# Layer 0 of a two-layer backbone: conv slice pieces ahead of retention, conv taps between the decay products

## The chip, the cores and the metric

One core of one Trainium2 chip. The metric is the device time of one execution in microseconds (us). The kernel before was run three times: 1911.14, 1915.06 and 1921.12 us, median 1915.06. Its profiled execution is a fourth one.

## The reference, cut to what matters

Two layers over 256 latent tokens and 256 context tokens with 1024 features. Each layer normalizes and modulates, projects once to three groups of heads, mixes each group, projects back, and adds; then comes a dense (layer 0) or an expert (layer 1) channel mixer. The three groups:

```
p = h @ w_in[l]                       # 2304 columns; the last 512 are conv value and conv gate
# retention, 4 heads of 64, for the latents and (layer 0 only) for the context:
a = einsum('bcihd,bcjhd->bchij', qc, kc) * dmat     # scores times a decay by distance
inner = einsum('bchij,bcjhe->bcihe', a, vc)
# conformer convolution, 256 channels, 31 taps:
h = a * sigmoid(gt)
h = conv_general_dilated(h, w, 31 taps, padding 15) + bias      # one filter per channel
h = silu(layernorm(h) * ln_w + ln_b)
# windowed attention with 8 query and 2 key/value heads
```

Layer 0 needs all of this for both streams (latents are stream 0, context is stream 1 in token order), layer 1 for the latents only. Everything is float32; a big product is made of three products of high and low parts (high x high, high x low, low x high).

## The kernel before, in words

Each engine has its own program, written out in order by hand, and semaphores between them. No planner orders anything: what stands first in an engine's program is done first.

**Banks.** Eight PSUM banks. VectorE empties banks 0 to 3 (VB), ScalarE banks 4 to 6 (AB), bank 7 (OB) is kept for attention. From the last slice of the input projection on, bank 3 is taken out of VectorE's ring and belongs to the conv slice, so three stay for the rest.

**The conv slice** (`conv_slice`, a Python generator of TensorE's program) makes the 512 conv columns with channels on the partitions. For each channel tile `ct` (128 channels each) it makes first the gate (half 1), then the value (half 0): four groups that all go through bank 3, each of 8 values of `k` with three matmuls each. It yields after every second `k`, so a group is four pieces and a piece is 6 matmuls of 512 columns; 16 pieces in all. The caller says with `next(conv)` where each piece goes. The first half of the rows of the weights is one item (`k` 0 to 3), the second half another; an item can be used when ScalarE has written its high part and VectorE its low part (`split_to`, the subtraction is line 1692). ScalarE empties a gate group with a sigmoid into SC (`conv_gate`), VectorE a value group by multiplying it with SC into the padded buffer CB (`conv_value`). Each group waits until the one before it has been emptied (semaphore `conv_gone`).

**Order of TensorE in layer 0**: projection slices; 2 pieces; `turn_heads`, the transposes of the conv filter and of the retention queries and keys (RT); 2 pieces; `states`, the decayed state of the context; 2 pieces; `retention`; `attention`. In `retention`, for each of the two streams: 1 piece, scores of heads 0 and 1, then for each head (with the scores of heads 2 and 3 ahead of head 1) 1 piece and `apply`, which multiplies the decayed scores AD of a head with its values. `apply` waits for VectorE's decay product of that head. Then `turn_qk` (transposes for attention) and the products with the states.

**Order of VectorE in layer 0**: the copies of the filter (convw) and of RT, the scaling of the decay table, the state copies, then for each stream four decay products `AD = scores * decay`, with `conv_value(0)` behind the first one, and taps behind some. A tap (line 1905) is one instruction over 512 tokens of 128 channels of the first channel tile (`CA = CB[shifted] * w + CA`), 31 in all, each waiting for the one before it. 17 taps stand behind decay products (9 behind head 3 of stream 0, 2 and 6 behind heads 1 and 3 of stream 1), 2 behind `conv_value(1)`, 12 in the first nine steps of attention (`TAPS`). The second channel tile is shared by ScalarE (products, line 1371) and GpSimd (adds, line 1663); it starts in attention and has no part in the change, though its adds run beside the taps. Behind the 14th add GpSimd computes the reciprocal roots for the retention readout (line 1624), for which VectorE's readout waits.

**Attention** is 16 steps `m` of two heads each in layer 0: scores (line 771), maximum on VectorE (line 2009), exponential on ScalarE, transposes (line 779), products with the values (line 790), and between them products with the modulation weights (line 561), whose 1 MB items arrive through four slots.

Of the kernel before, what the change touches and what calls it, by code (L numbers as in the profile page):

```python
# [43 lines left out]
PRODUCTS = 4  # L44
ADA_ITEMS = ((2, 1, 2, 1, 2, 1, 2, 1, 2, 2, 2, 2, 2, 2, 0, 0), (2, 3, 2, 3, 2, 2, 2, 0))
ADA_SLOTS = (0, 1, RAW, RAW + 1)
EARLY_TAPS = ({(0, 3): 9, (1, 1): 2, (1, 3): 6}, {(0, 1): 6, (0, 3): 10})
LAST_EARLY = (2, 3)
TAPS = ((2, 2, 2, 1, 1, 1, 1, 1, 1), (3, 3, 3, 3))
PRODUCT_TAPS = ((3, 3, 3, 3, 3, 3, 3, 3, 3, 3, 1), (6, 6, 6, 6, 6, 1))  # L50
READOUT = (1, 1)
CONV_TURN = (11, 6)
# [62 lines left out]
def build(nc, io, place):  # L115
    ctx = ExitStack()
    with ctx:
# [15 lines left out]
        _, YS_t = phase(("gap_ys", TT * D_MODEL, F32), ("YS", 2 * D_MODEL, F32R))  # L133
# [64 lines left out]
        for group, row_kb in ((0, 92), (1, 27), (2, 27)):  # L198
            _, row_t[group] = phase((f"gap_row{group}", row_kb * KB, F32), (f"row{group}", SLICE, F32))
        _, RT_t = phase(("gap_RT", 76 * KB, F32), ("RT", 8 * KB, F32))  # L200
        _, more0_t, _, more1_t = phase(("gap_more0", 104 * KB, F32), ("more0", 8 * KB, F32), ("gap_more1", 8 * KB, F32), ("more1", 8 * KB, F32))
        _, PT_t = phase(("gap_PT", 64 * KB, F32), ("PT", 8 * KB, F32))
        _, CA0_t = phase(("gap_CA0", 92 * KB, F32), ("CA0", 2 * KB, F32))
        _, distance_t = phase(("gap_distance", 80 * KB, F32), ("distance", 4 * KB, F32))
# [7 lines left out]
        _, heads_t, _, hTf_t, _, xn_t = phase(  # L212
            ("gap_heads", 96 * KB, F32), ("heads", 8 * KB, F32), ("gap_hTf", 24 * KB, F32), ("hTf", 16 * KB, F32),
            ("gap_xn", 12 * KB, F32), ("xn", 16 * KB, F32))

        _, SG_t, YG_t, _, HFr_t, HF_t = phase(
            ("gap_sg", 88 * KB, F32), ("SG", 4 * KB, F32), ("YG", 4 * KB, F32), ("gap_hfr", 32 * KB, F32),
            ("HFr", 44 * KB, F32R), ("HF", 4 * KB, F32))
# [6 lines left out]
        _, xnx_t = phase(("gap_xnx", 24 * KB, F32), ("xnx", 8 * KB, F32))  # L225
        _, hx0_t, _, hx1_t = phase(("gap_hx0", 88 * KB, F32), ("hx0", 4 * KB, F32), ("gap_hx1", 80 * KB, F32), ("hx1", 4 * KB, F32))
        _, hxc_t = phase(("gap_hxc", 72 * KB, F32), ("hxc", 8 * KB, F32))
# [254 lines left out]
        def _(pe):  # L482
# [220 lines left out]
                mm.then_inc(v_full, 1)  # L703

            def retention(layer, conv):
                pieces = 1 if layer == 0 else 2

                def scores(s, h):
                    b = open_v(("decayed", layer, s, h))
                    lo = 64 * (h % 2)  # L710
                    for jt in range(TT):
                        mm = nc.tensor.matmul(b[:, jt * SEQ:(jt + 1) * SEQ],
                                              RT[lo:lo + 64, 2 + h // 2, s * TT + jt, :],
                                              RT[lo:lo + 64, h // 2, s * TT:s * TT + TT, :].rearrange("p t n -> p (t n)"),
                                              start=True, stop=True)
                    mm.then_inc(v_full, 1)

                def apply(s, h, outs):
                    pe.wait_ge(v_done, job[("decayed", layer, s, h)] + 1)
                    for it in range(TT):  # L720
                        for jt in range(TT):
                            mm = nc.tensor.matmul(outs[it][:, h * 64:(h + 1) * 64],
                                                  AD[:, h, jt * SEQ + it * P:jt * SEQ + (it + 1) * P],
                                                  proj[:, s * TT + jt, C_RV + h * 64:C_RV + (h + 1) * 64],
                                                  start=(jt == 0), stop=(jt == TT - 1))
                        if h == RET_HEADS - 1:
                            mm.then_inc(a_full, 1)

                pe.wait_ge(v_done, n_v[0])
                for s in ((0, 1) if layer == 0 else (0,)):  # L730
                    for _ in range(pieces):
                        next(conv)
                    scores(s, 0)
                    scores(s, 1)
                    outs = [open_a(("inner", layer, s)), open_a()]
                    for h in range(RET_HEADS):
                        if h == 1:
                            scores(s, 2)
                            scores(s, 3)
                        for _ in range(pieces):  # L740
                            next(conv)
                        apply(s, h, outs)
                assert next(conv, None) is None
                turn_qk(layer)

                for t in range(TT):
                    b = open_v()
                    for pair in range(2):
                        mm = nc.tensor.matmul(b[:, pair * 256:(pair + 1) * 256], RT[:, pair, t, :], ST[:, pair, :],
                                              start=True, stop=True)  # L750
                    mm.then_inc(v_full, 1)
# [400 lines left out]
            for layer in range(DEPTH):  # L1152
                streams = (0, 1) if layer == 0 else (0,)
                if layer == 0:
                    after(cond_ready)
                    for i in range(2 * EARLY):
                        ada_product()
                        if i:
                            turn_normalized((0, 1), i - 1, i)
                    after(bias_in, 16)  # L1160
                    after(rows_out)
                    fold_rows(0)
                    turn_vectors()
                    turn_normalized((0, 1), KT - 1, KT)
                project_in(layer)
                conv = conv_slice(layer)
                next(conv), next(conv)
                turn_heads(layer)
                next(conv), next(conv)
                states()  # L1170
                next(conv), next(conv)
                retention(layer, conv)
                attention(layer)
                project_out(layer)
                if layer == 0:
                    dense_ffn()
# [68 lines left out]
        def _(act):  # L1245
# [229 lines left out]
            for layer in range(DEPTH):  # L1475
# [54 lines left out]
                def conv_gate(ct):  # L1530
                    act.wait_ge(conv_full, CONV_OUTS * layer + 2 * ct + 1)
                    nc.scalar.activation(SC[:, ct, 0:ncol], VB[3][:, 0:ncol], ACT.Sigmoid).then_inc(conv_gone, 1)
# [3 lines left out]
                gates = proj[:, 0:nt, C_RG:C_CONV]  # L1536
                nc.scalar.activation(gates, gates, ACT.Silu).then_inc(rg_ready, 1)
                conv_gate(0)
                if layer:
                    conv_gate(1)  # L1540
                for s in ((0, 1) if layer == 0 else (0,)):
                    for t in range(TT):
                        copy_out(RO[:, s * TT + t, :], take()[:, 0:256])
                    if layer == 0 and s == 0:
                        conv_gate(1)
                for t in tiles:
                    copy_out(AQT[:, :, t, :], take()[:, :].rearrange("p (r n) -> p r n", r=4))
                attention(layer, att_base + NT)
# [129 lines left out]
        def _(dve):  # L1678
# [16 lines left out]
            def take():  # L1695

                n = n_v[0]
                n_v[0] += 1
                dve.wait_ge(v_full, n + 1)
                return v_bank[n]  # L1700
# [8 lines left out]
            def copy_out(out, src):  # L1709
                nc.vector.tensor_copy(out, src).then_inc(v_done, 1)  # L1710
# [197 lines left out]
            def retention(layer, base):  # L1908
# [11 lines left out]
                def conv_value(ct):  # L1920
                    ns = 2 if layer == 0 else 1
                    dve.wait_ge(conv_full, CONV_OUTS * layer + 2 * ct + 2)
                    tt(CB[:, ct, 0:ns, CONV_WIDTH // 2:CONV_WIDTH // 2 + SEQ], VB[3][:, 0:ns * SEQ].rearrange("p (s n) -> p s n", s=ns),
                       SC[:, ct, 0:ns * SEQ].rearrange("p (s n) -> p s n", s=ns), ALU.mult).then_inc(conv_gone, 1)

                copy_out(convw[:, :, :], take()[:, 0:64].rearrange("p (c k) -> p c k", c=2)[:, :, 0:CONV_WIDTH])
                for t in tiles:
                    copy_out(RT[:, :, t, :], take()[:, :].rearrange("p (b n) -> p b n", b=4))

                after(dexp_out, 2)  # L1930
                nc.vector.tensor_scalar(dec[:, :], dec[:, :], HEAD_DIM ** -0.5, None, ALU.mult)
# [3 lines left out]
                step(nc.vector.memset(ST, 0.0))  # L1935
                nc.vector.tensor_copy(ST[0:64, :, 0:P], b[0:64, :].rearrange("p (c n) -> p c n", c=2)[:, :, 0:P])
                copy_out(ST[64:128, :, P:2 * P], b[64:128, :].rearrange("p (c n) -> p c n", c=2)[:, :, P:2 * P])
                after(pad_ready)
                for s in ((0, 1) if layer == 0 else (0,)):
                    if s:  # L1940
                        dve.wait_ge(a_full, full[("inner", layer, 0)] + 2)
                    for h in range(RET_HEADS):
                        tt(AD[:, h, :], take()[:, :], decay[:, h, :], ALU.mult).then_inc(v_done, 1)
                        if s == 0 and h == 0:
                            conv_value(0)
                        if (s, h) in EARLY_TAPS[layer]:
                            early_taps(EARLY_TAPS[layer][s, h])
                conv_value(1)
                early_taps(LAST_EARLY[layer])
                dve.wait_ge(att_done, base)  # L1950
                after(mask_in, 16)
# [416 lines left out]
```

## Time and profile before

| | us |
|---|---|
| median of 3 runs | 1915.06 |
| profiled execution | 1919.19 |
| its span, first to last instruction | 1917.4 |
| PE (TensorE matmul) busy | 1822.6 |
| DVE (VectorE) busy | 1339.3 |
| ACT (ScalarE) busy | 1050.9 |
| POOL (GpSimd) busy | 119.9 |

The names in the rows: PE is the matmul side of TensorE and PEld its weight load, DVE is VectorE, ACT is ScalarE, POOL is GpSimd. The retention of layer 0 lies at 138 to 167 us of the span, its attention from there to about 260 us. Busy shares over the whole span tell nothing of these stretches, which the windows show one by one.

### The profile page before, as it was taken

What the parts mean: (1) busy time and instruction counts of PE and PEld (TensorE: products, weight loads), DVE (VectorE), ACT (ScalarE), POOL (GpSimd) and SP (SyncE); (2) the same over time, 40 slices, a digit from 0 to 9 for tenths busy, and PEclk for the clock granted to TensorE, in tenths of its full rate; (3) what the DMA queues carried; (4) which work ended last, traced back from release to release, by engine and by line L of the source; (5) the groups of instructions that cost most, each with busy time, mean ns of one, the idle gap of its engine ahead of it and who ended that gap; (6) DMA issues with size and microseconds to landing.
All of it is one profiled execution on the core that took longest, in us unless ns stands there. A gap on an engine that the chain in (4) does not pass through costs nothing.

```text
span 1917.4 us, 23772 instructions
## 1 busy us (share of the span) xinstructions
PE 1822.6 (95%) x8964; PEld 1480.7 (77%) x8964; DVE 1339.3 (70%) x1280; ACT 1050.9 (55%) x1009; POOL 119.9 (6%) x126
## 2 busy tenths in 40 slices
PE   4999899999999999987999999999999999999996
PEld 2986578888888888576888788888888888888885
DVE  2579645333323367756888888889888898898886
ACT  3334644322222153545777776777776776777774
POOL 1123600000000012400000000000000000000000
PEclk8999989999999999997999999999999999999999
DMA  8325823532342234735999999999999999999994
GB/s 291 126 88 207 303 75 78 140 96 86 95 109 83 74 97 132 258 138 175 370 332 354 358 340 345 368 346 354 369 328 362 351 361 359 338 354 352 353 367 154
DMA packets 245911, 472.85 MB, mean 247 GB/s; under 512 B 10546, under 2 KB 60564, under 8 KB 245804
## 3 DMA queue, kind: packets, MB, share of 16 engines
q1 hardware_dynamic: 241712, 468.14, 68.9%
q10 hardware_dynamic: 4092, 3.20, 0.6%
q8 instruction: 77, 1.26, 0.3%
q14 instruction: 30, 0.25, 0.0%
HBM read 470.26 MB, written 1.05 MB: 246 GB/s over the span
## 4 chain that ended last, share of the span: by engine, by line
PE 48%; DMA 21%; DVE 16%; ACT 8%; issue 5%; POOL 2%; SPq 0%; DVEq 0%; ACTq 0%; POOLq 0%
PE bank L543 13%; PE bank L545 13%; PE bank L544 13%; DMA raw<-in_moe_w_gate_dram 10%; DVE parts L1707 9%; ACT parts L1409 6%; DMA raw<-in_moe_w_down_dram 5%; DMA raw<-in_moe_w_up_dram 4%; DMA raw<-in_ada_w_dram 2%; PE bank L561 1%; PE bank L1047 1%; POOL gb L1663 1%; DVE parts L1692 1%; PE bank L790 1%; DVE ACC L2180 1%
## 5 line engine op out<-in xcount | busy, mean ns | idle before, releaser
L1707 DVE TENSOR_TENSOR parts<-raw,parts 128x2048 fp32r<-128x2048 f32 x336 | 764.9, 2289 | 115.0 <-ACT parts L1409 113.9
L1409 ACT ACTIVATE parts<-raw 128x2048 fp32r<-128x2048 f32 x336 | 642.7, 1919 | 260.4 <-DMA raw<-in_moe_w_up_dram 94.9
L543 PE MATMUL bank<-parts,XEr 128*128 128x512 f32 x896 | 357.2, 399 | 8.7 <-DVE parts L1707 6.3
L545 PE MATMUL bank<-parts,XEr 128*128 128x512 f32 x896 | 350.1, 391 | 0.0
L544 PE MATMUL bank<-parts,XEr 128*128 128x512 f32 x896 | 349.4, 390 | 0.0
L1270 ACT ACTIVATE parts<-raw 128x2048 fp32r<-128x2048 f32 (+1 forms) x62 | 113.2, 1831 | 270.2 <-PE bank L545 250.0
L1692 DVE TENSOR_TENSOR parts<-raw,parts 128x2048 fp32r<-128x2048 f32 (+1 forms) x62 | 135.8, 2194 | 138.2 <-ACT parts L1270 137.9
L543 PEld LDWEIGHTS bank<-parts,XEr 128*128 128x128 f32 x896 | 168.7, 188 | 49.9 <-DVE parts L1707 10.3
L545 PEld LDWEIGHTS bank<-parts,XEr 128*128 128x128 f32 x896 | 168.5, 188 | 36.6
L544 PEld LDWEIGHTS bank<-parts,XEr 128*128 128x128 f32 x896 | 168.9, 188 | 32.6
L543 PE MATMUL bank<-parts,HTr 128*128 128x512 f32 x448 | 175.6, 392 | 1.3 <-DVE HTr L1707 0.8
L544 PE MATMUL bank<-parts,HTr 128*128 128x512 f32 x448 | 174.5, 390 | 0.0
L545 PE MATMUL bank<-parts,HTr 128*128 128x512 f32 x448 | 174.4, 389 | 0.0
L543 PE MATMUL bank<-hTr,parts 128*128 128x512 f32 (+1 forms) x432 | 164.1, 380 | 7.4 <-ACT hTf L1342 3.7
L544 PE MATMUL bank<-hTr,parts 128*128 128x512 f32 (+1 forms) x432 | 161.8, 375 | 0.0
L545 PE MATMUL bank<-hTr,parts 128*128 128x512 f32 (+1 forms) x432 | 161.8, 375 | 0.0
L543 PE MATMUL bank<-parts,hTr 128*128 128x512 f32 (+1 forms) x320 | 122.0, 381 | 7.3 <-DVE hTr L1707 3.3
L544 PE MATMUL bank<-parts,hTr 128*128 128x512 f32 (+1 forms) x320 | 120.3, 376 | 0.0
L545 PE MATMUL bank<-parts,hTr 128*128 128x512 f32 (+1 forms) x320 | 120.2, 376 | 0.0
L1707 DVE TENSOR_TENSOR HF<-bank,SG 128x512 f32<-128x512 f32 x22 | 15.2, 691 | 138.2 <-PE bank L545 138.2
L543 PEld LDWEIGHTS bank<-parts,HTr 128*128 128x128 f32 x448 | 84.1, 188 | 21.9 <-issue 2.0
L543 PEld LDWEIGHTS bank<-hTr,parts 128*128 128x128 f32 x432 | 81.9, 190 | 24.2 <-issue 7.2
(245 smaller groups left out, 2289.7 us busy)
## 6 DMA issues: line engine op xcount, KB each, us to landing
raw<-in_moe_w_gate_dram SPq DMA_DIRECT2D x112, 1024.0 KB, 7.2
raw<-in_moe_w_up_dram SPq DMA_DIRECT2D x112, 1024.0 KB, 7.2
raw<-in_moe_w_down_dram SPq DMA_DIRECT2D x112, 1024.0 KB, 6.7
raw<-in_ada_w_dram SPq DMA_DIRECT2D x28, 1024.0 KB, 8.0
more<-in_ada_w_dram SPq DMA_DIRECT2D x20, 1024.0 KB, 7.7
raw<-in_w_in_dram SPq DMA_DIRECT2D x12, 1024.0 KB, 5.1
raw<-in_ffn_w_gate_dram SPq DMA_DIRECT2D x22, 512.0 KB, 4.0
raw<-in_ffn_w_up_dram SPq DMA_DIRECT2D x22, 512.0 KB, 5.4
```

What stands on the lines that cost most here:

```text
L543: nc.tensor.matmul(out, st[0], mv[0], start=start, stop=False)
L544: nc.tensor.matmul(out, st[0], mv[1], start=False, stop=False)
L545: return nc.tensor.matmul(out, st[1], mv[0], start=False, stop=stop)
L561: mm = nc.tensor.matmul(b[32 * j:32 * j + 32, :], cond[:, half * KT // 2 + j, c0:c0 + 32], w[:, j, :], start=opening, stop=closing)
L790: mm = nc.tensor.matmul(OB[:, head * 64:(head + 1) * 64], PT[:, n % 4, kb * P:(kb + 1) * P], proj[:, kb, C_V + 64 * g:C_V + 64 * g + 64], ...
L1047: mm = nc.tensor.matmul(M[k // 4][:, (k % 4) * P:(k % 4 + 1) * P], xn[:, t, k * P:(k + 1) * P], PA[:, t, bass.ds(i * 2 + j, 1), :].rearran ...
L1270: nc.scalar.activation(parts[:, s, 0, 0:k * width], raw[:, r, 0:k * width], ACT.Copy).then_inc(hi_ready, 1)
L1409: nc.scalar.activation(parts[:, n % PARTS, 0, :], raw[:, r, :], ACT.Copy).then_inc(hi_ready, 1)
L1663: nc.gpsimd.tensor_tensor(acc, acc, CP[:, k % PRODUCTS, 0:ns, :], ALU.add).then_inc(pool_tap, 1)
L1692: nc.vector.tensor_tensor(parts[:, s, 1, 0:k * width], raw[:, r, 0:k * width], parts_f[:, s, 0, 0:k * width], ALU.subtract).then_inc(lo_re ...
L1707: return nc.vector.tensor_tensor(out, a, b, op)
L2180: nc.vector.scalar_tensor_tensor(acc, M[h][:, :], share[:, ee % 2, t:t + 1], acc, ALU.mult, ALU.add)\
```

## The change

In layer 0, 12 conv pieces stand ahead of retention (4 ahead of `turn_heads`, 4 ahead of `states`, 4 behind it), and retention has 4, all in its first stream: one ahead of the scores and one ahead of `apply` of heads 0, 1 and 2. Both sigmoids of the conv gate stand together in ScalarE's program. VectorE makes `conv_value(0)` right behind the copies of RT, and `conv_value(1)` behind head 3's decay product of stream 0. Taps stand behind every decay product: 3, 4, 4, 5 in stream 0 and 4, 4, 4, 1 in stream 1, then 2 more; none is left in attention. Layer 1 has the same order of instructions as before.

```diff
-EARLY_TAPS = ({(0, 3): 9, (1, 1): 2, (1, 3): 6}, {(0, 1): 6, (0, 3): 10})
+EARLY_TAPS = ({(0, 0): 3, (0, 1): 4, (0, 2): 4, (0, 3): 5, (1, 0): 4, (1, 1): 4, (1, 2): 4, (1, 3): 1}, {(0, 1): 6, (0, 3): 10})
-TAPS = ((2, 2, 2, 1, 1, 1, 1, 1, 1), (3, 3, 3, 3))
+TAPS = ((), (3, 3, 3, 3))
@@ retention, TensorE
-                pieces = 1 if layer == 0 else 2
+                between = iter((1, 1, 1, 1, 0, 0, 0, 0, 0, 0) if layer == 0 else (2, 2, 2, 2, 2))
...
-                    for _ in range(pieces):
+                    for _ in range(next(between)):
                         next(conv)
                     scores(s, 0)
                     scores(s, 1)
...
-                        for _ in range(pieces):
+                        for _ in range(next(between)):
                             next(conv)
                         apply(s, h, outs)
@@ layer loop, TensorE
-                next(conv), next(conv)
+                pieces = range(2 if layer else 4)
+                for _ in pieces:
+                    next(conv)
                 turn_heads(layer)
-                next(conv), next(conv)
+                for _ in pieces:
+                    next(conv)
                 states()
-                next(conv), next(conv)
+                for _ in pieces:
+                    next(conv)
@@ ScalarE
                 conv_gate(0)
-                if layer:
-                    conv_gate(1)
+                conv_gate(1)
...
-                    if layer == 0 and s == 0:
-                        conv_gate(1)
@@ retention, VectorE
                 for t in tiles:
                     copy_out(RT[:, :, t, :], take()[:, :].rearrange("p (b n) -> p b n", b=4))
+                if layer == 0:
+                    after(pad_ready)
+                    conv_value(0)
...
-                after(pad_ready)
+                if layer:
+                    after(pad_ready)
...
-                        if s == 0 and h == 0:
+                        if s == 0 and h == 0 and layer:
                             conv_value(0)
+                        if s == 0 and h == 3 and layer == 0:
+                            conv_value(1)
                         if (s, h) in EARLY_TAPS[layer]:
                             early_taps(EARLY_TAPS[layer][s, h])
-                conv_value(1)
+                if layer:
+                    conv_value(1)
```

## Rows read from the trace of the kernel before

**Rows 1.** The head of the page.

```profile
span 1917.4 us, 23772 instructions
```

**Rows 2.** Windows: PE, PEld, DVE, ACT, POOL busy us, PEclk, DMA share, GB/s.

```profile
138.00:151.00 13.00, 13.00 (x79) 10.62 (x78) 9.83 (x14) 0.77 (x2) 0.00 (x0) 1.00 0.01 1
151.00:162.00 11.00, 11.00 (x69) 9.13 (x69) 8.56 (x13) 0.60 (x1) 0.00 (x0) 1.00 0.00 0
...
180.00:195.00 15.00, 12.25 (x92) 6.77 (x91) 14.69 (x30) 11.16 (x29) 13.73 (x9) 1.00 1.04 384
```

**Rows 3.** Timeline: start us, us, engine, line, what; ahead of retention.

```profile
123.17 0.39 PE L543 MATMUL bank<-hTr,parts 128*128 128x512 f32 x1
...
125.66 0.39 PE L545 MATMUL bank<-hTr,parts 128*128 128x512 f32 x1
...
125.80 2.29 DVE L1692 TENSOR_TENSOR parts<-raw,parts 128x2048 fp32r<-128x2048 f32 x1 [4.19 <-ACT parts L1270]
...
128.28 1.26 PE L675 MATMUL bank<-const,proj 128*128 128x128 f32 x8 [0.96 <-DVE convw L1710]
```

**Rows 4.** Timeline of retention, to the first attention scores (L771).

```profile
138.03 1.14 PE L712 MATMUL bank<-RT 64*128 64x256 f32 x8
...
139.26 0.69 DVE L1707 TENSOR_TENSOR AD<-bank,decay 128x512 f32<-128x512 f32 x1 [3.63 <-PE bank L712]
...
144.01 0.55 DVE L1902 TENSOR_SCALAR CA<-CB,convw,vcols 128x512 f32<-128x512 f32 x1
...
144.59 6.26 DVE L1905 SCALAR_TENSOR_TENSOR CA<-CB,convw,CA 128x512 f32<-128x512 f32 x8
...
151.12 0.60 ACT L1532 ACTIVATE SC<-bank 128x512 f32<-128x512 f32 x1 [1.06 <-PE bank L545]
...
152.25 1.29 DVE L1707 TENSOR_TENSOR AD<-bank,decay 128x512 f32<-128x512 f32 x2 [1.40 <-PE bank L712]
...
161.42 1.09 PEld L722 LDWEIGHTS bank<-proj,AD 128*128 128x128 f32 x8
...
161.85 0.69 DVE L1707 TENSOR_TENSOR CB<-bank,SC 128x512 f32<-128x512 f32 x1 [0.27 <-PE bank L545]
...
166.50 0.76 PE L771 MATMUL bank<-AKT,heads 64*128 64x256 f32 x4
```

**Rows 5.** Groups by line from 168 to 212 us: count, busy us, mean ns, idle before.

```profile
L1905 DVE SCALAR_TENSOR_TENSOR CA<-CB,convw,CA 128x512 f32<-128x512 f32 x12 | 12.0, 999 | 0.1
```

**Rows 6.** The chain of waits in attention: start us, us, what.

```profile
175.21 1.28 POOL gb L1663
...
180.12 2.09 POOL gb L1663
...
187.65 1.68 POOL gb L1663
```

**Rows 7.** Timeline of attention, columns as in rows 3.

```profile
173.79 23.42 POOL L1663 TENSOR_TENSOR gb<-gb,QK 128x512 f32<-128x512 f32 x14 [54.58 <-ACT QK L1371]
...
197.59 2.91 POOL L1624 TENSOR_TENSOR lnr<-lnt,nhalf 128x16 f32<-128x16 f32 x1
...
200.53 2.28 DVE L1707 TENSOR_TENSOR RO<-RO,lnr 128x1024 f32<-128x1024 f32 x1 [4.47 <-POOL lnr L1624]
...
204.59 0.58 ACT L1356 ACTIVATE hTr<-bank 128x512 fp32r<-128x512 f32 x1
...
205.81 0.68 DVE L1707 TENSOR_TENSOR hTr<-bank,hTr 128x512 fp32r<-128x512 f32 x1
...
206.54 1.12 PE L779 MATMUL bank<-const,SC 128*128 128x128 f32 x4 [2.09 <-DVE hTr L1707]
```

**Rows 8.** Windows of 2 us, columns as in rows 2.

```profile
202.00:204.00 2.00, 0.67 (x2) 0.29 (x2) 1.90 (x7) 0.52 (x2) 1.93 (x1) 1.00 1.05 400
...
206.00:208.00 2.00, 1.46 (x8) 1.46 (x8) 2.00 (x2) 2.00 (x7) 1.86 (x2) 0.50 0.15 44
...
212.00:214.00 2.00, 2.00 (x12) 0.75 (x9) 1.79 (x2) 1.99 (x6) 1.86 (x2) 0.96 0.84 246
```

## The prediction

> **What bounds the kernel now.** I read the page first, for the span of the one profiled execution [rows 1], and then the windows, to find which engine is full where the change is made. From 138 to 162 us, layer 0's retention, TensorE is busy in every one of 24 us at the full clock, while VectorE is busy in 9.83 of the first 13 and 8.56 of the last 11 [rows 2]. So this stretch ends when TensorE has gone through its list. In the attention that follows it is the other way round: from 180 to 195 us VectorE is busy in 14.69 of 15 us and GpSimd in 13.73, TensorE in 12.25. The chain of waits puts that stretch on GpSimd: the adds of the second channel tile follow each other without a gap from 173.79 us, 14 of them in 23.42 us, then its power operation (2.91 us from 197.59), and VectorE waits 4.47 us for that before the readout's multiplication at 200.53 [rows 7]. From 206.54 us TensorE is dense again. All the weights of later layers are asked for when earlier ones are used up, so I take a delay here as passed on to the end in full.
>
> **What the change does to the order.** TensorE issues the same instructions; 13 instead of 7 conv pieces (6 matmuls each) now stand ahead of the first scores, 3 instead of 9 behind them. VectorE runs the same 31 taps, but 28 instead of 17 ahead of the last decay product of retention, 3 instead of 2 behind it, none instead of 12 in attention. Layer 1 keeps its order.
>
> **Term 1, the way to the first decay product.** Twelve matmuls go from 123.17 to 125.66 us, first to last start, so one costs 0.226 us and a piece 1.36 us [rows 3]. Six more pieces: +8.15 us. The third and fourth piece are now issued ahead of the head transposes, and they read the second half of the conv weights, whose low part VectorE finishes at 125.80 + 2.29 = 128.09 us; TensorE would go on at 125.89, so it stands for 2.2 us in a place where it used to do the transposes. In return the transposes no longer wait for the convw copy, which stands behind that same split on VectorE: -0.96 us [rows 3]. The thirteenth piece is the first of the fourth group and needs the conv bank emptied by the sigmoid (0.60 us, [rows 4]); nothing stands between it and the twelfth now. The end of the last matmul (0.39 - 0.23), 0.60 and two handovers make 0.86 us of standing. Other new waits are covered: the fifth piece's sigmoid by the transposes, the ninth's product on VectorE by the state matmuls. VectorE's scaling of the decay table and the state copies come behind that product, about 3 us of work, under four pieces (5.4 us) of TensorE. Sum: 8.15 + 2.2 - 0.96 + 0.86 = +10.25 us; the first decay product moves from 139.26 to about 149.5 us. I give this +-1.
>
> **Term 2, from the first to the last product.** Now VectorE's list is the longer one. A tap costs 6.26 / 8 = 0.78 us, the first one 0.58, a product 1.29 / 2 = 0.645, the gating product 0.61 (161.85 to the next start) [rows 4]. In order: 28 taps (0.58 + 27 x 0.78 = 21.7), 8 decay products (5.2) and one gating product (0.6): 27.5 us. TensorE has 3 pieces, 4 pairs of scores at 1.1 us and 7 applications at about 1.1 us in the same time, 16 us, each ready before VectorE comes to the product that reads it, so it hides behind VectorE and waits. The last product ends at 149.5 + 27.5 = 177.0, and the last application starts at 177.1 instead of 161.42: +15.7 us. In the stretch before, the idle third of VectorE paid for 19 taps; now the idle comes first (while 13 pieces run) and can't be used, as the first tap stands behind the first product in program order.
>
> **Term 3, the tail.** From the last application to the first scores of attention it is 5.08 us (161.42 to 166.50) [rows 4]. The last three taps lie beside it. But TensorE comes to this tail rested: in the second stream it works about 4 us in 14, in stretches of 1 to 2 us between waits of up to 3. The trace has a like case: after waits of 2.2 and 2.1 us with a burst between them (0.67 us busy from 202 to 204) the granted clock stands at 0.50 from 206 to 208, the lower level, 1.2 GHz, and is back by 212 to 214, at 0.96 [rows 8]. If it is low through the tail, some 5.6 us of wall time do half the work: +2.8 us at most. If it happens to be high, 0. I take +2.0, nearer to the like case. The Trainium skill ("TensorE: Matmul & The Clock Gate", Part 1) puts the fall down to an idle engine and the return to sustained work. By it alone, waits broken by bursts might keep the clock up, and the sum would be 2.0 smaller; the trace shows a fall after broken waits.
>
> **Term 4, what attention gives back.** The 12 taps take 12.0 us of VectorE there, 1.00 us each instead of 0.78 [rows 4, 5]. They would be worth all of it if VectorE set the end, but it stands 4.5 us for GpSimd at 200.5, so what counts is how much earlier GpSimd's fourteenth add ends. An undisturbed add has a pitch of 175.21 - 173.79 = 1.42 us; fourteen would take 19.9 instead of 23.42, a surplus of 3.5 [rows 6, 7]. Two of the adds are stretched from 1.28 to 2.09 beside the readout's 1024 wide operations, which stay: 1.6. The rest, 1.9 us, is that of the taps (an add beside one takes 1.68) [rows 6]. After it one more tap pair stands ahead of the low part at 205.81, whose high part ScalarE has at 204.59 + 0.58 = 205.17, and TensorE's next transposes wait for it until 206.54 [rows 7]: 0.6 us. Together -2.5 us. Bounds: nothing, if the modulation weights' transfers set the pace instead (DMA share 1.04 from 180 to 195 [rows 2]); -12.0, if VectorE did. Behind 206.54 TensorE is the bound and the last three taps of attention are free. The Trainium skill ("SBUF — State Buffer", SBUF: two separate sides) says that a VectorE instruction with two SBUF inputs and a GpSimd one that reads SBUF exclude each other for a whole instruction. The trace agrees in kind (1.28 grows to 1.68 and 2.09), but by that rule the nine taps ahead of the fourteenth add would return 9 x 0.78 = 7.0 us instead of 1.9 (an estimate from that page's rule), and the chain holds a surplus of only 3.5.
>
> **Sum.** 15.7 + 2.0 - 2.5 = +15.2 us. The profiled execution took 1919.19 us around a span of 1917.4 [rows 1]; it would become 1934.4. The median of the three runs, 1915.06, is 4.1 lower, and by that the forecast is 1930.3 us. Of this the 15.7 is sure within 1.5, as it is counted out of repeated rows.
>
> **Rivals.**
> Attention gives back everything, not slower than before. VectorE is full from 180 to 195, its little scale instructions there grow too, and if it, not GpSimd, sets the pace, 12.0 us of taps go and with them some 3 us of stretched small operations. Then 15.7 + 0 - 15.0 = +0.7, 1915.8 us. It decides at the readout's multiplication: if VectorE no longer finds itself waiting for the power operation there, this is the case. Against it stands that wait of 4.5 us in the trace of before, which any time saved on VectorE alone would only lengthen. 6 in 100.
> The port is given back in full (the rule above, as a mechanism here): each of nine taps had kept GpSimd for 0.78: 15.7 + 2.0 - 7.0 - 0.6 = +10.1, 1925.2 us. Against it: the surplus in the chain. 7 in 100; a mixture of this and the first rival somewhere near 1921, another 6.
> The clock doesn't fall in the second stream: 15.7 - 2.5 = +13.2, 1928.3 us. 22 in 100.
> Transfers hold the attention: four modulation slots are full at its start as before, but if GpSimd lets go earlier, TensorE meets weights that haven't landed. Then nothing is given back: 15.7 + 2.0 = +17.7, 1932.8 us. 15 in 100. With a clock that falls again in attention up to 1936. 4 in 100.
> The forecast itself, 40 in 100, from 1928 to 1933.
>
> **How the numbers follow.** All cases from the clock rival to the transfers lie at +12 to +19; below them lie 19 in 100, of which the port case is inside. So the range is 1922 to 1936. A measurement of this kernel can't tell less than 0.5%, 9.6 us, from nothing. Slower than 1924.6: the forecast, clock and transfers (81) and most of the port case (5), 86 in 100. Within 0.5%: the first rival, the mixture and the rest of the port case, 14. I take 2 and 1 off these for a mechanism that I don't see, by which it would be faster: 84, 13 and 3.
>
> **What would show it.** In the profile after: TensorE idle for about 2 us near 126 to 128; the first decay product near 149.5; from there to about 179.5 a VectorE without a gap and TensorE with waits for decay products of 2 to 3 us, their sum about 12; granted clock below 1 somewhere from 165 to 182; the first attention scores near 182 to 185 instead of 166.5; fourteen GpSimd adds in about 21.5 us instead of 23.4. I am wrong if the first product comes by 145, if taps between products cost less than 0.78, or if the distance from the first attention scores to the dense part (40 us before) shrinks by more than 5.

## The result and the profile after

The changed kernel is slower: median 1933.12 us (five runs, 1926.80 to 1936.10) against 1913.76 us (five runs, 1911.14 to 1921.12), ratio 1.0085 with a 95% interval of 1.0064 to 1.0106, so +16.3 us (12 to 20) on 1913.76. The two medians by themselves are 19.4 us apart, inside that interval. Forecast was +15.2, 1930.3 us, slower.

The profiled execution of the changed kernel took 1926.80 us, the fastest of its five; its span is only 7.6 us longer than before's. So the spans of two profiles don't give the size. The stages do. First the timeline around retention, which answers to rows 3 and 4 (start us, us, engine, line, what):

```profile
126.20 2.29 DVE L1693 TENSOR_TENSOR parts<-raw,parts 128x2048 fp32r<-128x2048 f32 x1 [4.20 <-ACT parts L1274]
...
128.55 0.50 PE L543 MATMUL bank<-hTr,parts 128*128 128x512 f32 x1 [2.10 <-DVE parts L1693]
...
147.27 0.47 PE L543 MATMUL bank<-hTr,parts 128*128 128x512 f32 x1 [0.78 <-ACT SC L1536]
...
149.99 0.69 DVE L1708 TENSOR_TENSOR AD<-bank,decay 128x512 f32<-128x512 f32 x1 [7.11 <-PE bank L712]
...
153.35 3.10 DVE L1906 SCALAR_TENSOR_TENSOR CA<-CB,convw,CA 128x512 f32<-128x512 f32 x4
...
160.73 1.10 PE L722 MATMUL bank<-proj,AD 128*128 128x64 f32 x8 [2.52 <-DVE AD L1708]
...
165.83 1.94 PE L722 MATMUL bank<-proj,AD 128*128 128x64 f32 x8 [2.00 <-DVE AD L1708]
...
172.98 1.97 PE L722 MATMUL bank<-proj,AD 128*128 128x64 f32 x8 [1.29 <-DVE AD L1708]
...
175.86 0.68 DVE L1708 TENSOR_TENSOR AD<-bank,decay 128x512 f32<-128x512 f32 x1
176.46 2.32 DVE L1906 SCALAR_TENSOR_TENSOR CA<-CB,convw,CA 128x512 f32<-128x512 f32 x3
...
176.60 1.97 PE L722 MATMUL bank<-proj,AD 128*128 128x64 f32 x8 [1.65 <-DVE AD L1708]
...
184.31 0.75 PE L771 MATMUL bank<-AKT,heads 64*128 64x256 f32 x4
```

VectorE stands for 7.11 us ahead of the first decay product, at 149.99 instead of 139.26, and from there runs product, taps, product, taps to 178.8 without a gap. TensorE waits for products, and an application takes 1.94 to 1.97 us in the second stream; in the kernel before it takes 1.00, as in the last one there:

```profile
161.65 1.00 PE L722 MATMUL bank<-proj,AD 128*128 128x64 f32 x8
```

The windows of the changed kernel show why (busy us of PE, PEld, DVE, ACT, POOL, PEclk, DMA share, GB/s):

```profile
155.00:160.00 5.00, 3.22 (x23) 2.70 (x21) 4.86 (x8) 0.00 (x0) 0.00 (x0) 1.00 0.26 74
160.00:165.00 5.00, 3.10 (x16) 2.18 (x16) 4.86 (x9) 0.77 (x2) 0.00 (x0) 0.68 0.91 345
165.00:170.00 5.00, 4.17 (x18) 3.28 (x18) 4.86 (x9) 0.00 (x0) 0.00 (x0) 0.50 0.00 0
170.00:175.00 5.00, 3.65 (x16) 3.27 (x16) 4.86 (x7) 0.00 (x0) 0.00 (x0) 0.50 0.00 0
175.00:180.00 5.00, 3.40 (x16) 3.40 (x17) 3.67 (x6) 1.30 (x3) 0.00 (x0) 0.50 0.00 0
180.00:185.00 5.00, 5.00 (x28) 4.18 (x26) 1.97 (x3) 1.85 (x4) 0.00 (x0) 0.77 0.02 3
```

VectorE is at 4.86 of 5, TensorE at 3.1 to 3.2 of 5. A window of 1 us, below, has the granted clock fall just ahead of 162, behind the wait of 2.52 us and the application after it; from there it is at 0.50, 1.2 GHz, until it rises again at about 182:

```profile
161.00:162.00 1.00, 1.00 (x10) 0.93 (x11) 0.97 (x3) 0.51 (x2) 0.00 (x0) 0.92 1.02 365
```

Now attention, which answers to rows 7:

```profile
191.59 21.52 POOL L1664 TENSOR_TENSOR gb<-gb,QK 128x512 f32<-128x512 f32 x14 [71.98 <-ACT QK L1375]
213.19 0.21 POOL L1624 TENSOR_SCALAR lnt<-lnv 128x16 f32<-128x16 f32 x1
213.48 2.91 POOL L1625 TENSOR_TENSOR lnr<-lnt,nhalf 128x16 f32<-128x16 f32 x1
...
216.42 2.28 DVE L1708 TENSOR_TENSOR RO<-RO,lnr 128x1024 f32<-128x1024 f32 x1 [7.29 <-POOL lnr L1625]
...
221.84 1.31 PE L779 MATMUL bank<-const,SC 128*128 128x128 f32 x4 [1.15 <-DVE hTr L1708]
...
244.66 1.13 PE L771 MATMUL bank<-AKT,heads 64*128 64x512 f32 x4
```

The fourteen adds take 21.52 instead of 23.42 us, and VectorE, freed of its taps, waits longer for GpSimd: 7.29 instead of 4.47 us [rows 7].

To compare kernels I use the start of the scores of step 12 of attention, in a part where TensorE is dense in all of them: 229.64 us before, 244.66 after, +15.0. Of this 0.40 us is there ahead of all changed code: the split of the conv weights' second half (L1692, in the changed kernel L1693) starts at 126.20 instead of 125.80 [rows 3]. Counted from the split, step 12 is 14.6 us later. Behind it the code is unchanged. GpSimd's clearing of the accumulator ahead of the experts stands at 886.72 before and 904.68 after, +18.0: 3 us more came in without a changed instruction. In the timeline of the changed kernel:

```profile
904.68 1.80 POOL L1675 MEMSET ACC<- 128x2048 f32 x1 [10.33 <-DVE top L1708]
```

From there to the end it was 1030.7 us before and 1020.3 after. In the eight experiments, which all have the same code there, this last part took between 1022.4 and 1035.0 us in one profile each. That spread, not the change, is what separates the two spans' difference of 7.6 from the stage's 15.

### The profile page after: what moved, and what is told of

The parts are those of the page before. It is cut to its first block, busy times and chain, and to the rows that moved or that the text cites. A ratio compares the mean times of both kernels' runs of the same rounds, so it can differ in the third digit from the quotient of the medians.

```text
span 1925.0 us, 23773 instructions
## 1 busy us (share of the span) xinstructions
PE 1828.7 (95%) x8964; PEld 1491.7 (77%) x8964; DVE 1333.5 (69%) x1280; ACT 1051.4 (55%) x1009; POOL 117.3 (6%) x126
## 3 DMA queue, kind: packets, MB, share of 16 engines
HBM read 470.26 MB, written 1.05 MB: 245 GB/s over the span
## 4 chain that ended last, share of the span: by engine, by line
PE 82%; DVE 7%; DMA 3%; ACT 3%; issue 2%; POOL 2%; SPq 0%; DVEq 0%; ACTq 0%; POOLq 0%
PE bank L543 24%; PE bank L544 24%; PE bank L545 24%; PE bank L1047 2%; DMA raw<-in_ada_w_dram 2%; PE bank L561 2%; PE bank L1101 1%; DMA raw<-in_moe_w_gate_dram 1%; DVE parts L1693 1%; DVE parts L1708 1%; PE bank L790 1%; POOL gb L1664 1%; DVE CA L1906 1%; ACT parts L1413 1%; PE bank L779 1%
## 5 line engine op out<-in xcount | busy, mean ns | idle before, releaser
L1693 DVE TENSOR_TENSOR parts<-raw,parts 128x2048 fp32r<-128x2048 f32 (+1 forms) x62 | 135.7, 2193 | 138.8 <-ACT parts L1274 138.5
L544 PE MATMUL bank<-parts,HTr 128*128 128x512 f32 x448 | 174.5, 390 | 0.0
L1708 DVE TENSOR_TENSOR HF<-bank,SG 128x512 f32<-128x512 f32 x22 | 15.2, 691 | 138.2 <-PE bank L545 138.2
```

Source lines behind the costliest of these rows:

```text
L544: nc.tensor.matmul(out, st[0], mv[1], start=False, stop=False)
L1693: nc.vector.tensor_tensor(parts[:, s, 1, 0:k * width], raw[:, r, 0:k * width], parts_f[:, s, 0, 0:k * width], ALU.subtract).then_inc(lo_re ...
L1708: return nc.vector.tensor_tensor(out, a, b, op)
```

## The experiments

They ran in two groups of four, each group on one chip with runs of the kernel before between them (16 and 23), against which the ratios are taken; heads_early and after_ro10 ran only once. The table has, from the profiles, the start of the first decay product, the end of the last one, the first attention scores, and the scores of step 12 (its difference to before), the same difference counted from each profile's own split, then the ratio over all runs.

| kernel | first product | last product ends | first scores | step 12 | from the split | whole kernel |
|---|---|---|---|---|---|---|
| before | 139.26 | 156.98 | 166.50 | 229.64 | 0 | 1 |
| after | 149.99 | 176.54 | 184.31 | 244.66 (+15.0) | +14.6 | 1.0085 [1.0064, 1.0106] |
| pieces_only | 149.76 | 170.62 | 180.52 | 243.82 (+14.2) | +14.0 | 1.0066 [1.0044, 1.0088] |
| taps_only | 139.53 | 167.17 | 172.17 | 233.47 (+3.8) | +3.5 | 1.0023 [1.0007, 1.0038] |
| fill_waits | 150.18 | 176.74 | 181.75 | 243.53 (+13.9) | +13.3 | 1.0070 [1.0040, 1.0101] |
| heads_early | 149.64 | 176.21 | 184.00 | 244.45 (+14.8) | +14.5 | one run |
| taps_ahead | 148.94 | 168.49 | 175.86 | 237.62 (+8.0) | +8.6 | 1.0067 [1.0046, 1.0088] |
| after_ro10 | 150.04 | 176.59 | 184.59 | 244.65 (+15.0) | +14.5 | one run |
| before_ro10 | 139.79 | 157.51 | 167.03 | 229.22 (-0.4) | -0.9 | 0.9987 [0.9968, 1.0006] |
| best | 139.05 | 156.77 | 166.29 | 227.39 (-2.3) | -2.0 | 0.9989 [0.9975, 1.0004] |

The split itself starts between 125.16 and 126.41 us, with the same code ahead of it in all ten profiles, so a bare start can be off by more than 1 us. Counted from the split, the first product repeats: 13.45 to 13.48 us in the four kernels with the pieces as before, 23.76 to 23.79 in five of the six with the pieces in front.

**pieces_only**: which half of the change costs?

```diff
-EARLY_TAPS = ({(0, 0): 3, (0, 1): 4, (0, 2): 4, (0, 3): 5, (1, 0): 4, (1, 1): 4, (1, 2): 4, (1, 3): 1}, {(0, 1): 6, (0, 3): 10})
-TAPS = ((), (3, 3, 3, 3))
+EARLY_TAPS = ({(0, 3): 9, (1, 1): 2, (1, 3): 6}, {(0, 1): 6, (0, 3): 10})
+TAPS = ((2, 2, 2, 1, 1, 1, 1, 1, 1), (3, 3, 3, 3))
```

> The changed kernel with the taps back where the kernel before has them (9, 2 and 6 behind products, 2 behind the last value, 12 in attention); only the 12 pieces in front, the two sigmoids together and the places of the two gating products stay. Theory (VectorE's serial list after a late first product): first decay product near 150.0 as in the changed kernel; TensorE done with the first stream by 159; VectorE waits for the fourth conv group until 157.3, then 9 taps to 165, products of stream 1 with 2 taps between, the last one done near 169.5; first attention scores near 174.5 to 176 (before 166.5, changed 184.3); attention from its first scores to those of step 9 in 46 us as before; step 9 at +8 to +9.5, whole kernel +8 to +10 us. Rival (the taps between the products alone make the loss, pieces in front cost only their stalls of 2 us): first attention scores near 169, whole kernel +2 to +3.

First product and the taps up to 164.5 came as expected, but the first scores at 180.5 instead of 174.5 to 176, and the pieces alone cost +14.2 us, nearly the whole loss. The expectation left out the clock. Timeline and windows of this kernel:

```profile
165.34 1.94 PE L722 MATMUL bank<-proj,AD 128*128 128x64 f32 x8 [5.43 <-DVE AD L1708]
...
169.23 5.38 PE L722 MATMUL bank<-proj,AD 128*128 128x64 f32 x24
```
```profile
160.00:165.00 5.00, 0.00 (x0) 0.00 (x0) 4.82 (x7) 0.00 (x0) 0.00 (x0) 0.67 0.86 323
165.00:170.00 5.00, 4.66 (x20) 3.76 (x20) 2.88 (x6) 0.00 (x0) 0.00 (x0) 0.50 0.00 0
170.00:175.00 5.00, 5.00 (x25) 5.00 (x25) 4.82 (x8) 0.73 (x2) 0.00 (x0) 0.50 0.00 0
```

The block of nine taps holds the first product of stream 1 back, TensorE stands idle for 5.43 us, wakes at half its clock, and has four applications, a pair of scores and the transposes of the tail still before it, with no long wait between them to absorb that. That the clock makes the difference is read from these windows; fill_waits tests it on the changed kernel, no run does on this one.

**taps_only**: the other half.

```diff
-EARLY_TAPS = ({(0, 3): 9, (1, 1): 2, (1, 3): 6}, {(0, 1): 6, (0, 3): 10})
-TAPS = ((2, 2, 2, 1, 1, 1, 1, 1, 1), (3, 3, 3, 3))
+EARLY_TAPS = ({(0, 0): 3, (0, 1): 4, (0, 2): 4, (0, 3): 5, (1, 0): 4, (1, 1): 4, (1, 2): 4, (1, 3): 1}, {(0, 1): 6, (0, 3): 10})
+TAPS = ((), (3, 3, 3, 3))
```

> The kernel before with only the taps moved (3, 4, 4, 5, 4, 4, 4, 1 behind the products, then 2), pieces as before. Theory: first product at 139.3 as before; VectorE's list from there is 26.6 us of taps and products plus some 1.5 us of waits for the first value and for scores, last product done near 167.7 instead of 157.0, last application there instead of 161.4; first attention scores near 172.9, up to 2 more if the clock falls; attention to step 9 2.5 us shorter than before; step 9 at +4 to +6, whole kernel +4 to +6 us. Rival (the taps in attention are worth their 12 us, or hide in retention): whole kernel -2 to -6.

As the theory had it: last product at 167.2, first scores at 172.2, +3.8 us at step 12, +4.4 (1.3 to 7.3) as a whole. The rival is excluded. Counted from the split the two halves would add to 17.5; together they make 14.6. With the pieces in front the taps cost only 0.6 more, since retention is then late by VectorE's list in either case and attention is 2.5 shorter.

**fill_waits**: is the long tail the clock?

```diff
+FILL = ((0, 0, 0, 10), (9, 6, 10, 10))
...
+                        if layer == 0:
+                            for _ in range(FILL[s][h]):
+                                nc.tensor.matmul(OB[:, :], hTr[:, 0, 0, 0:P], hTr[:, 0, 0, :], start=True, stop=True)
                         apply(s, h, outs)
```

> The changed kernel with 45 matmuls of 512 columns that nobody reads, in TensorE's program ahead of the last application of stream 0 (10) and those of stream 1 (9, 6, 10, 10), into the attention bank, which is free there; each about 0.23 us, so they fill the waits for decay products. Theory (term 3 is the lower clock of 1.2 GHz after those waits): granted clock 1.00 from 162 to 184, last application to first attention scores 5.1 us instead of 7.7, first scores near 181.8 instead of 184.3, the rest as in the changed kernel: 2.5 us less, +12 to +14 against before. Rival (the tail is longer because of VectorE's last taps or of the copies, not the clock): still 7.5 us or more, and the fillers only add.

```profile
165.00:170.00 5.00, 4.44 (x28) 3.17 (x27) 4.89 (x8) 0.00 (x0) 0.00 (x0) 1.00 0.00 0
170.00:175.00 5.00, 4.83 (x28) 3.94 (x28) 4.82 (x8) 0.00 (x0) 0.00 (x0) 1.00 0.02 3
...
215.00:220.00 5.00, 2.58 (x5) 0.71 (x6) 3.85 (x9) 3.45 (x11) 4.57 (x4) 0.69 1.03 382
220.00:225.00 5.00, 5.00 (x26) 2.57 (x26) 4.76 (x7) 3.30 (x7) 4.57 (x4) 0.50 0.10 39
```
```profile
176.80 1.10 PE L723 MATMUL bank<-proj,AD 128*128 128x64 f32 x8
...
181.75 0.76 PE L775 MATMUL bank<-AKT,heads 64*128 64x256 f32 x4
```

The clock stays at 1.00 through retention, an application takes 1.10 us, and from the last one to the first scores it is 4.95 instead of 7.71 us. So 2.8 us of the loss is the clock and no wait; taps_only, at full clock there, has the same 4.95. At step 12 1.3 us of this gain are left (from the split), because the clock falls in attention, for longer than in the changed kernel; over the whole kernel, +13.4 us (7.7 to 19.4), the gain can't be told from none.

**heads_early**: are the stalls of term 1 what they were taken for?

```diff
-                for _ in pieces:
+                for _ in range(2):
                     next(conv)
                 turn_heads(layer)
-                for _ in pieces:
+                for _ in range(2 if layer else 6):
                     next(conv)
```

> The changed kernel with the head transposes behind the second conv piece as in the kernel before (2 pieces, transposes, 6 pieces, states, 4 pieces). Theory (term 1): the wait of 2.1 us for the low part of the second half of the conv weights goes, the 0.96 us wait in the transposes comes back: first decay product 1.1 to 1.4 us earlier than in the changed kernel, near 148.7, and everything behind it by as much, first attention scores near 183. Rival (another wait, VectorE's copies and decay scaling, comes last there): first product stays at 149.8 or later.

A miss. The 2.10 us wait for the low part goes, but the first product comes only 0.2 us earlier, counted from the split (23.58 instead of 23.79 us), and not 1.1 to 1.4:

```profile
128.54 1.25 PE L675 MATMUL bank<-const,proj 128*128 128x128 f32 x8 [0.97 <-DVE convw L1711]
133.22 0.50 PE L543 MATMUL bank<-hTr,parts 128*128 128x512 f32 x1 [0.69 <-ACT SC L1536]
146.92 0.47 PE L543 MATMUL bank<-hTr,parts 128*128 128x512 f32 x1 [0.78 <-ACT SC L1536]
```

The 0.97 for the filter copy is back, and the fifth piece now waits 0.69 for the first sigmoid, which the transposes had covered. I had reckoned with the first and not with the second: 2.10 - 0.97 - 0.69 = 0.44, still 0.2 more than was gained. The rival, by which another wait comes last, has half of the case: it is another wait, though TensorE's for the sigmoid and none for VectorE's copies.

**taps_ahead**: the idle of VectorE ahead of the first product.

```diff
+                else:
+                    early_taps(EARLY_TAPS[0][0, -1])
...
+EARLY_TAPS = ({(0, -1): 9, (0, 0): 2, (0, 1): 2, (0, 2): 3, (0, 3): 4, (1, 0): 3, (1, 1): 2, (1, 2): 3, (1, 3): 1}, {(0, 1): 6, (0, 3): 10})
```

> The changed kernel with 9 of the 31 taps moved ahead of the first decay product (behind the state copies), the rest 2, 2, 3, 4, 3, 2, 3, 1 behind the products and 2 at the end; pieces as in the changed kernel. Theory (the loss is VectorE's serial list of taps and products after a first product at 150, while VectorE stands for 7.1 us ahead of it): the 9 taps fill those 7 us, the first product stays near 150.0, the last is done 9 x 0.775 = 7 us earlier, near 169.5 instead of 176.5; first attention scores near 176.5 (clock low) or 174.5 (clock high) instead of 184.3; whole kernel +7 to +9 us against before. Rival (TensorE's own order and its lower clock set the stretch once the pieces are in front, as with the taps put back, where it came to 180.5): first attention scores 179 or later, whole kernel +11 or more.

```profile
142.45 6.26 DVE L1906 SCALAR_TENSOR_TENSOR CA<-CB,convw,CA 128x512 f32<-128x512 f32 x8
148.94 0.69 DVE L1708 TENSOR_TENSOR AD<-bank,decay 128x512 f32<-128x512 f32 x1 [0.23 <-PE bank L712]
...
168.55 1.97 PE L722 MATMUL bank<-proj,AD 128*128 128x64 f32 x8 [1.67 <-DVE AD L1708]
```

The nine taps vanish in the wait (7.11 becomes 0.23) and the last product ends 8.1 us earlier, of which 1.05 is the earlier start of this profile: 7.0 as worked out. First scores at 175.9, step 12 at +8.0 (+8.6 from the split): in the stages the theory holds. The whole kernel gives +12.8 us (8.8 to 16.9), which is outside the expected +7 to +9 except for the lower end of its interval, and within the rival's +11 or more; the rival's own sign, scores at 179 or later, did not come. What the other 4 to 5 us are, or whether they are chance in four runs, is open: the accumulator's clearing is at +9.4, so they are not in the stages that were changed.

**after_ro10** and **before_ro10**: what of GpSimd holds attention?

```diff
-RO_TAP = (14, 13)
+RO_TAP = (10, 13)
```

> The changed kernel with GpSimd's power operation for the readout behind its 10th add instead of its 14th. Theory (GpSimd's chain up to this operation sets attention's pace, term 4): VectorE's wait there falls from 7.3 us to about 1.5, and the distance from the first attention scores to the transposes behind the low part (37.5 us) shrinks by 2 to 5 us. Rival (the adds themselves, through ScalarE's products, hold it): the distance stays within 1 us of 37.5.

> The kernel before with GpSimd's power operation behind its 10th add instead of its 14th. Theory: VectorE's wait of 4.5 us at the readout's multiplication goes; ScalarE then meets the adds 11 to 13 three us later, so of the 4.5 us 2 to 3.5 are gained: first attention scores to the transposes 36.5 to 38 us instead of 40.0, whole kernel -2 to -3.5 us. Rival (VectorE, full from 180 to 195, sets the pace): 39.5 us or more, whole kernel 0.

Both fell short. In after_ro10 VectorE's wait for the power operation went from 7.29 to 1.59 us, and step 12 came at 244.65, as without: its rival held. In before_ro10 the wait is gone, but the first scores are followed by the transposes behind the low part after 39.3 us (167.03 to 206.34), 0.7 less than before, where 2 to 3.5 were expected and the rival had 0.5 or less; step 12 is 0.9 us earlier (from the split). The wait only showed where GpSimd's chain was met. In after_ro10 ScalarE stands at the adds instead, and VectorE waits 5.29 us for ScalarE's high part, where it waited 1.05 in the changed kernel. So the number of GpSimd instructions ahead of a step counts and not which of them comes first:

```profile
211.17 2.29 DVE L1708 TENSOR_TENSOR RO<-RO,lnr 128x1024 f32<-128x1024 f32 x1 [1.59 <-POOL lnr L1625]
...
221.50 0.69 DVE L1708 TENSOR_TENSOR hTr<-bank,hTr 128x512 fp32r<-128x512 f32 x1 [5.29 <-ACT hTr L1360]
```
```profile
212.41 0.72 ACT L1375 ACTIVATE QK<-CB,convw 128x512 f32<-128x512 f32 x1 [2.29 <-POOL gb L1664]
214.62 0.72 ACT L1375 ACTIVATE QK<-CB,convw 128x512 f32<-128x512 f32 x1 [1.48 <-POOL gb L1664]
```

**best**: the kernel before, with two more taps in retention, none in steps 7 and 8 of attention, and the power operation earlier.

```diff
-EARLY_TAPS = ({(0, 3): 9, (1, 1): 2, (1, 3): 6}, {(0, 1): 6, (0, 3): 10})
-TAPS = ((2, 2, 2, 1, 1, 1, 1, 1, 1), (3, 3, 3, 3))
-RO_TAP = (14, 13)
+EARLY_TAPS = ({(0, 3): 10, (1, 1): 3, (1, 3): 6}, {(0, 1): 6, (0, 3): 10})
+TAPS = ((2, 2, 2, 1, 1, 1, 1), (3, 3, 3, 3))
+RO_TAP = (10, 13)
```

> The kernel before with the power operation behind the 10th add and two taps more in retention (10, 3 and 6 behind the products, 2 at the end; attention 2, 2, 2, 1, 1, 1, 1 and none in steps 7 and 8). The taps take idle time of VectorE in retention (1.4 and 0.7 us of waits for scores), so first attention scores stay at 166.5 to 167; no tap stands ahead of the low part in step 7: 0.6 us more than the power operation alone. Whole kernel -2.5 to -4.5 us against before. Rival: the taps delay products that TensorE waits for, first scores at 168 or later, and the gain is under 1.5.

The two taps cost nothing in retention (first scores 166.29), and step 12 is 2.0 us earlier (from the split). Twelve runs give 0.9989, -2.1 us, with an interval that holds 1, where 2.5 to 4.5 us less were expected: it beats the changed kernel and can't be told from the kernel before.

## Why the prediction was right

Point by point, from the two profiles, without the 0.40 us that are there ahead of all changed code.

| step | predicted us | measured us |
|---|---|---|
| term 1, first product | +10.25 | 149.99 - 139.26 - 0.40 = +10.3 |
| term 2, first to last product | 27.5 | 176.54 - 149.99 = 26.6 |
| last application | +15.7 | 176.60 - 161.65 - 0.40 = +14.6 |
| term 3, tail | +2.0 | 7.71 - 4.85 = +2.9 |
| term 4, attention to the transposes | -2.5 | 37.53 - 40.04 = -2.5 |
| sum | +15.2 | +14.9 at the transposes, +14.6 at step 12 |

(161.65 is the start of the matmuls of before's last application, 4.85 us ahead of its first scores. The prediction took the start of its weight load, 161.42, so 0.23 us stand in another row there.)

**Term 1** held to 0.1, with its waits visible as 2.10 and 0.78 us. **Term 2** was taken 0.9 too long: a group of four taps is followed by its product after 3.02 us (153.35 to 156.37), 0.755 a tap, where I took 0.78 from the length of a group that includes the last tap's end, and 27 of these make 0.7. Two counts beside it were wrong, and neither enters the sum: in the kernel before 11 taps, not 17, stand ahead of the last decay product and 8 behind it, since the last six follow head 3 of stream 1; and three pairs of scores, not four, come behind the first product. **Term 3** was set between high and low clock and came out fully low, as the case of waits of 2.1 and 2.2 us in before had shown [rows 8]; the rival by which the clock doesn't fall is excluded by the windows. fill_waits made that rival's case: +13.3 at step 12 from the split, where it had 13.2. The last application came 1.1 us less late than forecast and the tail grew 0.9 us more. That these errors cancel is luck, and without it the sum would be 1 us off. The 0.3 us by which step 12 is less late than the transposes are not explained.

**Term 4** came out in both its parts: the adds gave back 1.9 us, and from the readout's multiplication to the transposes it is 5.42 instead of 6.01 us, 0.6 less. The runs that carry the same change repeat the whole: first scores to the transposes (L779 with VectorE's low part as releaser) is 40.04 us before and 40.03 in pieces_only, both with taps in attention, and 37.53 after and 37.66 in taps_only, both without (220.55 - 180.52; 209.83 - 172.17). The three other runs without taps in attention and with the power operation in its place, fill_waits, heads_early and taps_ahead, have 37.49 to 37.70. So the 12 taps, 12.0 us of VectorE, are worth 2.5 us. The two rows, of pieces_only and of taps_only:

```profile
220.55 1.11 PE L779 MATMUL bank<-const,SC 128*128 128x128 f32 x4 [2.09 <-DVE hTr L1708]
```
```profile
209.83 1.31 PE L779 MATMUL bank<-const,SC 128*128 128x128 f32 x4 [1.50 <-DVE hTr L1707]
```

This excludes the rivals by which VectorE sets the pace (15.0), the shared access gives back 7.6, or transfers hold attention and nothing comes back. A clock that falls in attention made no difference between the two: it is low for a stretch in either, 0.53 in the window from 205 to 210 before and 0.50 from 220 to 225 after.

The adds show what a tap costs GpSimd, and that the prediction counted it wrongly. Four of the ten taps ahead of the fourteenth add were done before the first add began, so six ran beside the adds and not nine; the last two of them start at 190.69 and 195.33. Taps of the kernel before, one of its adds, then the long adds of the changed kernel, whose other adds up to the fourteenth take 1.27 to 1.32:

```profile
176.42 2.43 DVE L1905 SCALAR_TENSOR_TENSOR CA<-CB,convw,CA 128x512 f32<-128x512 f32 x2
...
182.34 1.82 DVE L1905 SCALAR_TENSOR_TENSOR CA<-CB,convw,CA 128x512 f32<-128x512 f32 x1
...
187.45 0.74 DVE L1905 SCALAR_TENSOR_TENSOR CA<-CB,convw,CA 128x512 f32<-128x512 f32 x1
```
```profile
182.34 1.28 POOL gb L1663
```
```profile
194.41 2.17 POOL gb L1664
...
199.58 2.16 POOL gb L1664
```

So the two adds beside the readout's wide operations stay long, as the prediction had it, and those beside taps became short: 23.42 became 21.52, 1.9 us for six taps, and not the 7.0 that the prediction worked out for nine from the rule of the Trainium skill ("SBUF — State Buffer", SBUF: two separate sides). With six taps it would have been 4.7. The rule itself is not refuted by this: the tap at 187.45 ends at 188.19, 0.54 us behind the start of the add at 187.65 [rows 6], and that add took 1.68 instead of 1.28 us, 0.40 more and not the tap's whole 0.74; and the tap at 182.34, which starts together with an add of 1.28 us, took 1.82 instead of 0.74. In both rows the loss, 0.40 and 1.08 us, is within what was left of the other instruction. The prediction's 7.0 had charged the whole length of each tap.

My reason for term 4 stands with a correction from after_ro10: GpSimd's chain does hold this stretch, but not through the power operation in particular. The sign in the prediction for the rival, VectorE no longer waiting at the readout, came out the other way: it waited 7.29.

**The chain between the terms** was told right but for one number: TensorE's waits for products sum to 7.5 us, not 12, because at half clock the work between them takes twice as long: the two pairs of scores and the three applications behind the clock's fall, up to the last wait, took 10.0 us instead of the 5.3 that they take at 1.14 and 1.00 us each.

**What I had not seen** is how the halves divide. The prediction charged the pieces with the late start (10.25) and the taps with the longer list. pieces_only shows that the pieces alone cost 14.0 us (from the split), since nine taps in one block then do the harm that the spread ones do; after a first product that is 10 us late, VectorE's order hardly matters unless taps move ahead of it (taps_ahead: 7 us).

The whole kernel's +16.3 (12 to 20) holds both 15.2 and the stage's 14.6. The 18.0 at the experts' start is within what single profiles scatter there: taps_only stands at +3.8 at step 12 and at +1.7 there (888.41), before_ro10 at -0.4 and at +1.7 (888.37), and after_ro10, at +15.0 at step 12 like the changed kernel, at +15.2 (901.92).

## What to carry to other kernels

When work of one engine is moved ahead of a point, ask which other engine starts its serial list at that point: here TensorE's 8 us of moved work are no work more, but they put off by 10 us the start of a list of 27 us on VectorE, which stood idle meanwhile for 7.11 us. Freeing an engine that is 98% busy can be worth a fifth of its time, if the chain of waits in the same stretch runs through another; VectorE's 12.0 us gave 2.5. And a change of 15 us in a span of 1917 is read from stages, each counted from a mark ahead of the changed code, since one unchanged stage alone moved by up to 15 us between profiles.

## What the runs showed of the hardware that I had not expected

The granted clock went to 0.50 in the changed kernel at about 162 us, behind a wait of 2.52 us that began in a window in which TensorE was still busy for 3.22 of 5 us, and stayed there through windows with 4.17, 3.65 and 3.40 busy of 5 at that level; it came back in the dense tail, near 182. In taps_only, with TensorE busy for at least 3.93 of each 5 us from 150 to 170, it stayed at 1.00, and so it did through retention in fill_waits, with the waits filled. Waits that cost nothing on the chain can so double the work behind them: 2.8 us here, and, by its windows, part of the 5 us by which pieces_only came later than expected. The other is the price between VectorE and GpSimd: an add that began 0.54 us ahead of a tap's end took 1.68 instead of 1.28 us, and a tap that began together with an add took 1.82 instead of 0.74.
